# Norms x3 and x4 by halves of the tokens, residual added by matmul, and attention's values and scores in a new order

## The reference

```python
def second_block(x, ...):
    h = x
    for i in range(2):
        mix = gated_deltanet(h, ...) if i == 0 else moba_attention(h, b_w_qkv, b_w_out)
        h = layer_norm_2(ALPHA * h + mix, ln1_g[i], ln1_b[i])                       # x3, x5
        h = layer_norm_2(ALPHA * h + swiglu(h, f_w13[i], f_w2[i]), ln2_g[i], ln2_b[i])  # x4, output
    return h

def swiglu(x, w13, w2):
    g, u = split(x @ w13, 2)
    return (silu(g) * u) @ w2            # hidden width 2816 = 22 x 128

# attention at 256 tokens: 8 heads of 128; rotary on the first 32 dimensions of q and k;
# s = q k^T / sqrt(128), causal; p = softmax(s); o = p v; out = o @ w_out
```

## Time and profile before

| | |
|---|---|
| runs | 1166.37, 1163.05, 1165.20 us; median 1165.2 |
| profiled execution, on the device | 1170.1 us |
| its span, from first to last instruction | 1168.3 us |
| busy PE / PEld / DVE / ACT | 1115.2 / 1066.6 / 802.1 / 614.5 us |
| matmul records | 8328 |
| mean granted TensorE clock | 0.971 of full speed |
| read from memory | 192.9 MB, 166 GB/s over the span |

### The profile page before, as it was taken

How to read it: one execution, slowest core, us unless ns; L and a number is a source line. 1 busy time by engine, 2 the same in 40 slices (tenths; PEclk the granted TensorE clock), 3 DMA queues, 4 the chain that set the end, 5 groups by cost and what they waited for, 6 DMA issues and landing times.

```text
span 1168.3 us, 20107 instructions
## 1 busy us (share of the span) xinstructions
PE 1115.2 (95%) x8328; PEld 1066.6 (91%) x8328; DVE 802.1 (69%) x1355; ACT 614.5 (53%) x1029; POOL 3.3 (0%) x13
## 2 busy tenths in 40 slices
PE   7998989999999998879989999999999999999997
PEld 7998879899999988779989999999999787999996
DVE  7987478878787787486665665555579737555555
ACT  6567435465556547843344454545455546445453
POOL 0000000000000000000000000000000000000000
PEclk8999979999999998889989999999999999999999
DMA  9985246347766623143223265555526424555520
GB/s 374 418 316 166 86 145 252 109 157 244 246 209 203 205 72 127 26 130 134 73 91 100 67 218 194 186 194 188 191 76 201 158 101 157 200 192 181 196 75 37
DMA packets 58554, 195.56 MB, mean 167 GB/s; under 512 B 10848, under 2 KB 11232, under 8 KB 58208
## 3 DMA queue, kind: packets, MB, share of 16 engines
q1 hardware_dynamic: 58464, 194.28, 48.8%
HBM read 192.94 MB, written 1.31 MB: 166 GB/s over the span
## 4 chain that ended last, share of the span: by engine, by line
PE 75%; DVE 16%; ACT 6%; issue 2%; DMA 1%; SPq 1%; ACTq 0%; DVEq 0%
PE ps L534 62%; DVE lo L1639 4%; PE ps L809 4%; ACT hi L1106 2%; DVE raw L1626 2%; PE ps L636 2%; PE ps L541 1%; DVE B L1648 1%; DVE ev L1877 1%; PE ps L553 1%; DVE ev L1874 1%; DVE st L1656 1%; PE ps L691 1%; PE ps L815 1%; DVE B L1661 1%
## 5 line engine op out<-in xcount | busy, mean ns | idle before, releaser
L1639 DVE TENSOR_TENSOR lo<-raw,hi 128x1024 fp32r<-128x1024 f32 x311 | 377.8, 1222 | 170.0 <-ACT hi L1106 169.2
L534 PE MATMUL ps<-hh,hi 128*128 128x256 f32 x1664 | 478.2, 287 | 14.2 <-DVE hl L1673 3.2
L534 PE MATMUL ps<-hl,hi 128*128 128x256 f32 x1664 | 471.5, 283 | 0.0
L534 PE MATMUL ps<-hh,lo 128*128 128x256 f32 x1664 | 471.1, 283 | 0.0
L1106 ACT ACTIVATE hi<-raw 128x1024 fp32r<-128x1024 f32 x311 | 324.4, 1052 | 62.9 <-PE ps L534 62.6
L534 PEld LDWEIGHTS ps<-hh,hi 128*128 128x128 f32 x1664 | 320.0, 192 | 18.6 <-issue 8.7
L534 PEld LDWEIGHTS ps<-hl,hi 128*128 128x128 f32 x1664 | 320.0, 192 | 1.0
L534 PEld LDWEIGHTS ps<-hh,lo 128*128 128x128 f32 x1664 | 319.8, 192 | 0.0
L534 PE MATMUL ps<-fh,hi 128*128 128x256 f32 x392 | 111.4, 284 | 3.5 <-ACT B L1210 2.5
L534 PE MATMUL ps<-fl,hi 128*128 128x256 f32 x392 | 110.2, 281 | 0.0
L534 PE MATMUL ps<-fh,lo 128*128 128x256 f32 x392 | 110.1, 281 | 0.0
(11 more groups left out here) (280 smaller groups left out, 1283.1 us busy)
## 6 DMA issues: line engine op xcount, KB each, us to landing
raw<-in_w SPq DMA_DIRECT2D x359, 512.0 KB, 4.1
B<-in_t SPq DMA_DIRECT2D x2, 512.0 KB, 4.4
xa<-in_x SPq DMA_DIRECT2D x1, 1024.0 KB, 11.2
B<-in_r SPq DMA_DIRECT2D x1, 1024.0 KB, 5.5
out<-h SPq DMA_DIRECT2D x4, 256.0 KB, 2.0
cst<-in_c SPq DMA_DIRECT2D x1, 864.0 KB, 9.1
B<-between SPq DMA_DIRECT2D x32, 4.0 KB, 1.6
vec<-in_v SPq DMA_DIRECT2D x1, 328.5 KB, 7.5
```

The costliest lines, as they stand in the source:

```text
L534: m = g.matmul(o, l, r, start=first and n == 0, stop=last and n == 2, skip_group_check=True)
L1639: g.tensor_tensor(lo[:, j % SPLIT, :], raw[:, PLACE[j] % RAW, :], hi[:, j % SPLIT, :].bitcast(F), ALU.subtract).then_inc(*up("lo", j))
```

## The change

- **Norms x3 and x4** are made by `norm_tokens` as x5 is, on all engines; `after`, `residual` and the filler matmuls inside go. The second feed-forward layer becomes `ffn_tokens` with eight new units `w13r0`. `high` and `low` of the third last `w20` unit + AHEAD are added at its end, as units follow it in the plan.
- **gout**: the residual x2 is multiplied into banks 0 to 3 (`residual_in`) after the last `gdn` tile, then the eight units are done by tokens, units 5 to 7 for c = 0 first.
- **Banks**: in the delta rule banks 0 to 3 and 4 to 7 change places.
- **Attention**: after x4, `absorb` with `vt` 0 to 3 only; then tiles 0 to 11, `scores` 0 and 1, tiles 12 and 13, `scores` 2 and 3, tiles 14 and 15, `scores` 4 and 5, `vt` 4 and 5, `scores` 6 and 7, `vt` 6, `turned` 0 and 1, `vt` 7, `turned` 2 and 3, `apply` 0, `turned` 4, `apply` 1, `turned` 5, all of `carry_in`, then `bout`. A table `ATT` fixes the rotation of the four banks. ScalarE loads the Exp table after the copy of tile 11 and does `exps` between the copies. On VectorE the copies of the values stand behind `weights` 6 and 7.

The diff, cut to its core:

```diff
+ATT = ([("tile", n) for n in range(12)] + [("s", 0), ("s", 1), ("tile", 12), ("tile", 13), ("s", 2), ("s", 3)]
+       + [("tile", 14), ("tile", 15)] + [("s", n) for n in (4, 5, 6, 7)] + [("t", n) for n in range(4)]
+       + [("a", 0), ("t", 4), ("a", 1), ("t", 5), ("a", 2), ("t", 6), ("a", 3), ("t", 7)] + [("a", n) for n in (4, 5, 6, 7)])
+ATT_BANK = {what: 4 + i % 4 for i, what in enumerate(ATT)}
...
+    w += [("vt", k) for k in range(4)] + [("qkv", t) for t in range(16)] + [("vt", k) for k in range(4, 8)]
+    w += [("bout", k) for k in range(8)]
+    w += swiglu(1)
...
-BY_TOKENS = ("x5",)
+BY_TOKENS = ("x3", "x4", "x5")
...
+            def residual_in():
+                for n in (21, 22, 23):
+                    s.wait_ge(*at("conv4", n))
+                s.wait_ge(*at("qss", 2))
+                for k in range(8):
+                    carry_in("x2", k)
+
             def gout(k):
-                rows_in("gout", k, 4, xh[:, k, :], xl[:, k, :], at("gl", k // 2), k == 0, k == 7,
-                        [at("conv4", n) for n in (21, 22, 23)] + [at("qss", 2)] if k == 0 else [])
+                for n, cs in [(k, (0, 1) if k < 5 else (0,))] + ([(5, (1,)), (6, (1,)), (7, (1,))] if k == 7 else []):
+                    rows_out_of("gout", n, (fh if n < 4 else hh)[:, n, :], (fl if n < 4 else hl)[:, n, :], at("gl", n // 2), cs,
+                                n == 7)
...
-            after("x3", lambda k: at("res", ("x3", k - k % 2)))
-            ffn("w130", "w20", "x3", at("hl", ("x3", 0)))
-            after("x4", lambda k: at("res", ("x4", k - k % 2)))
+            ffn_tokens("w130", "w20", "w13r0", "x3", [[at(*core_bank.out[4 + 2 * c + half]) for half in range(2)] for c in range(2)])
+
+            absorb("vt", "x4", [[at("ff_out", ("w130", 2 * FF - 4 + 2 * c + half)) for half in range(2)] for c in range(2)])
...
+            for n in range(12):
+                qk_tile(n)
+            for hd in (0, 2):
+                scores(hd)
+                scores(hd + 1)
+                qk_tile(12 + hd)
+                qk_tile(13 + hd)
+            scores(4)
+            scores(5)
+            vt(4)
+            vt(5)
+            scores(6)
+            scores(7)
+            vt(6)
             turned(0)
             turned(1)
+            vt(7)
+            turned(2)
+            turned(3)
+            apply(0)
+            turned(4)
+            apply(1)
+            turned(5)
+            for k in range(8):
                 carry_in("x4", k)
...
# ScalarE
+                high(UNIT[kdown, FF - 3] + AHEAD)
...
+            for n in range(16):
+                high(UNIT["qkv", n] + AHEAD)
+                s.wait_ge(*at("unit", UNIT["qkv", n]))
+                dst = qq[:, n, :] if n < 8 else kk_[:, n - 8, :]
+                g.activation(dst, bank[ATT_BANK["tile", n]][:, 0:S], ACT.Copy).then_inc(*up("qk_out", n))
+                if n == 11:
+                    table(ACT.Exp)
+                if n in (13, 15):
+                    exps(n - 13)
+                    exps(n - 12)
+            high(UNIT["vt", 4] + AHEAD)
+            high(UNIT["vt", 5] + AHEAD)
+            exps(4)
+            exps(5)
+            high(UNIT["vt", 6] + AHEAD)
+            exps(6)
+            exps(7)
             turned(0)
             turned(1)
+            high(UNIT["vt", 7] + AHEAD)
+            turned(2)
+            turned(3)
...
# VectorE
+            for n in range(16):
+                low(UNIT["qkv", n] + AHEAD)
+                if n in (2, 4, 6, 8):
+                    rope(qq, n - 2)
+                if n in (12, 14):
+                    scores(n - 12)
+                    scores(n - 11)
+                if n in (10, 12, 14):
+                    rope(kk_, n - 10)
+                if n == 14:
+                    weights(0)
+                    weights(1)
+            low(UNIT["vt", 4] + AHEAD)
+            scores(4)
+            scores(5)
+            rope(kk_, 6)
+            weights(2)
+            weights(3)
+            low(UNIT["vt", 5] + AHEAD)
+            low(UNIT["vt", 6] + AHEAD)
+            scores(6)
+            scores(7)
+            weights(4)
+            weights(5)
+            low(UNIT["vt", 7] + AHEAD)
+            weights(6)
+            weights(7)
             s.wait_ge(*at("unit", UNIT["vt", 7]))
             for b in (2, 3):
                 g.tensor_copy(vv[:, 1, (b - 2) * 512:(b - 2) * 512 + 512], bank[b][:, :]).then_inc(*up("v_v", b))
-            weights(6)
-            weights(7)
```

More of the change, by code:

```diff
@@ L741, in absorb @@
                 for k in range(4):
[L742 to L745, removed]
+                    tokens_unit(kind, nid, k, 1)
             def ffn_tokens(kup, kdown, kr, nid, frees):
@@ L1094, in tensor @@
                 bout(k, (1,))
-            ffn_tokens("w131", "w21", "w13r1", "x5", [[at(*a_free[4 + 2 * c + half]) for half in range(2)] for c in range(2)])
+            ffn_tokens("w131", "w21", "w13r1", "x5", [[at("att_lo", 4 + 2 * c + half) for half in range(2)] for c in range(2)])
         def scalar(g, s):
@@ L1524, in gout @@
             def gout(k):
-                high(UNIT["gout", k] + AHEAD)
+                if k < 6:
+                    high(UNIT["gout", k] + AHEAD)
             def nothing(*a):
@@ L1560, in exps @@
                              accum_out=x[:, 3:4]).then_inc(*up("exp", (hd, 1)))
[L1562 to L1576 removed]
             def turned(hd):
[L1579 removed]
+                b = ATT_BANK["t", hd]
                 s.wait_ge(*at("probT_mm", hd))
@@ L2194, in gout @@
             def gout(k):
-                low(UNIT["gout", k] + AHEAD)
+                if k < 6:
+                    low(UNIT["gout", k] + AHEAD)
             def nothing(*a):
@@ L2203, in vector @@
                          "gate": gate, "gturn": gturn, "gout": gout})
-            def after(nid, kind, gain, bias, i, parts=True, b0=0):
-                residual(nid, kind, b0)
-                center(nid, xa, 8, B[0], B[1], 4)
-                root(nid)
-                if parts:
-                    norm_parts(nid, B[1], veccol(gain, i), veccol(bias, i), xa)
-                else:
-                    norm_out(nid, 8, B[1], veccol(gain, i), veccol(bias, i), xa)
-            after("x3", ("gout", 7), "ln1_g_2", "ln1_b_2", 0, b0=4)
-            ffn("w130", "w20", False)
-            after("x4", ("w20", FF - 1), "ln2_g_2", "ln2_b_2", 0)
+            norm_tokens("x3", ("gout", 7), veccol("ln1_g_2", 0), veccol("ln1_b_2", 0), UNIT["w13r0", 2])
+            ffn_tokens("w130", "w20", "w13r0")
+            norm_tokens("x4", ("w20", FF - 1), veccol("ln2_g_2", 0), veccol("ln2_b_2", 0), UNIT["vt", 2])
+            for k in range(4):
+                low(UNIT["vt", k] + AHEAD)
             def rope(dst, n):
```

232 lines of the change are left out of this document (80 added, 152 removed).

## The result

| | before | after |
|---|---|---|
| median of the runs, us | 1164.77 (1161.14 to 1167.33, 6 runs) | 1157.33 (1154.6 to 1161.26, 6 runs) |
| profiled execution, us | 1170.11 | 1159.28 |
| its span, us | 1168.3 | 1157.5 |
| its mean granted clock | 0.971 | 0.979 |

The ratio is 0.9939, with a 95% interval of 0.9912 to 0.9966: faster by 7.4 us. The prediction was 7.3 us, from 1165.2 to 1157.9.

A forecast was written before the change was run, and what follows sets the result against it. TensorE's queue was taken as the bound. Residual +3.5, norm x3 with second layer -5.5, norm x4 -10.8 and attention +5.5 gave -7.3 us, from 1165.2 to 1157.9, with an 8-in-10 range of 1151.5 to 1165.0.

The forecast's parts named there:

- Residual x2: Ahead of `gout`: carrying the residual into the banks is hidden by nothing, +3.5 us, at most 5.2 at partly lower clock.
- lower clock outside attention: Sign of being wrong: the profile after shows TensorE's clock lowered anywhere but in attention; no size given.
- `gout` by halves: Delta rule's output: units 5 to 7 emitted by halves, eight units of 12 matmuls as before, cost nothing.
- Norm x3 and the second layer: Second feed-forward layer and its norm take the last layer's form and time: 197.7 becomes 192.2 us, -5.5.
- norm x4: Norm before attention: 13.88 us becomes 3.1, with values units 0 to 3 covering the second half, -10.8.
- Attention: Same work in a new order, 106.1 us; waits of 7.0 plus slow clock 2.8, less 4.3 before: +5.5 us.
- The waits: TensorE idle before `scores` 2, 4, 6 and `apply` 0 in attention: 1.6, 0.3, 1.6 and 3.6 us, together 7.0.
- The slow clock behind the fourth: Attention, behind the wait before `apply` 0: 2.8 us lost, as after a wait of 3.42 us.
- The table: ScalarE's change to Exp in attention: 1.80 us with the copy before; a drain would make the first wait 1.3 longer.
- B: Rival, chance 0.15: the wait before `apply` 0 is not there, giving 1151.5 us.
- C: Rival: clock falls at unfilled turns x3, x4 and both 1.6 us waits; 1164.9 us (chance 0.17) or 1169.1, slower (0.06).
- D: Rival, chance 0.04: halves do not hide norms x3 and x4, head start of 4.2 us lost twice, +8.4, 1166.3.

The follow-up runs named there:

- experiment 4: Kernel after without the 32 matmul records that carry residual x2 into the banks of `gout`, so the output lacks it: 1153.28 us, ratio 0.9912.
- experiment 11: Kernel after, unchanged, run again: 1155.39 us, ratio 0.9925.
- experiment 5: Kernel after with the last three units of `gout` and `w20` made for both token halves together instead of half 0 first: 1164.23 us, ratio 1.0006.
- experiment 2: Kernel after with all sixteen key and query tiles first, then `vt` 4 to 7 each with two `scores`, and early value copies: 1150.69 us, ratio 0.9893.
- experiment 6: Kernel before without the 14 and 38 idle matmuls in norms x3 and x4: 1169.2 us, ratio 1.005.
- experiment 7: Kernel of experiment 2 with the carry of residual x4 ahead of `apply` 0 instead of behind `turned` 5: 1149.52 us, ratio 0.9883.
- experiment 10: Kernel after with the Exp table loaded behind tile 12 instead of tile 11: 1155.37 us, ratio 0.9929.
- experiment 1: Kernel after with the value copies ahead of `weights` 6 and 7 on VectorE and of `turned` 2 and 3 on ScalarE: 1151.34 us, ratio 0.9899.
- experiment 3: Kernel after with 24 filler matmuls in the wait before `apply` 0: 1155.98 us, ratio 0.9932.
- experiment 8: Kernel of experiment 7 with filler matmuls at four waits of the delta rule, 26 of them before kk(0): 1147.28 us, ratio 0.9862.
- experiment 9: Kernel of experiment 8 without the 26 filler matmuls before kk(0): 1147.95 us, ratio 0.9862.

## Why the prediction was right, step by step

- **Residual x2, +3.5.** Right: 3.7 by experiment 4. In the profile after, the carry itself took 5.20 at a clock of 0.67, the upper bound that was given. It is no further loss: the slow stretch behind the wait had fallen on `gout` 0 in the kernel before. When the clock stayed up (experiment 11), the stretch of `gout` took 32.31. The clock below 1.00 at this place is not the "lower clock outside attention" that the prediction named as a sign of being wrong: it was there before.
- **"`gout` by halves: nothing."** Off by 0.3. A unit of one half gives its follower 1.4 us of cover instead of 2.8, and `gout` 6 waits 0.26 us for its own `hl` part, which VectorE makes just in time.
- **Norm x3 and the second layer, -5.5; norm x4, -10.8.** Right to 0.1: taking the last layer as the measure of the second was sound, since its form and queue order are the same. Experiment 5 shows that 7.2 of it rest on the head start of half 0, and experiment 2 that these two, with the residual, are worth 11.7 (9.0 to 13.6) by the time of the runs too. The other edits in the norms, the tokens' form and the next layer's units for one half at a time, were not tried apart. One reading was loose: of the 13.00 us busy in the norm not most were fillers, but about half (7.00 are left in experiment 6).
- **Attention, +5.5.** 5.2 measured, but the terms were less good than their sum. The waits were 1.51, none, 1.54 and 3.27 us (predicted 1.6, 0.3, 1.6, 3.6): 6.3 instead of 7.0. The slow clock behind the fourth cost 1.7 us (3.35 us at 0.58 and the next 3.7 at 0.92), not 2.8: the term was taken from the stretch behind 3.42 us, which lasted longer. That stretch is a poor measure in any case: behind the same wait the clock stayed at 1.00 in experiments 2, 7, 10 and 11 (last section). Against these 1.8 too much stand 1.5 too little in the work: 104.40 less 6.3 and 1.7 is 96.4 for what was summed up as 94.9 (106.1 less four units). Experiments 1 and 2 say the same, 107.4 and 107.3 for the 106.1. Of it 0.9 can be seen: two units between two pairs of `scores` take 5.98 us (896.58 to 902.56) and not 5.60, three times over, 1.1 in all; the `scores` themselves take 0.58, 0.07 less than counted, 0.6 in all; and the first twelve tiles take 34.0 instead of 33.6. Nearly all of the 0.38 lies at the two changes of kind: from the last start of a tile to the first of `scores` it is 0.31 (902.25 to 902.56), from the first start of a tile behind `scores` to its second 0.30 (896.58 to 896.88), where inside a tile it is 0.12. The two errors had opposite signs, and the total owes its 0.3 to that.
- **The table.** 1.40 us from the load to the next `hi` (887.35 to 888.75), 1.80 from the copy before, as in the earlier trace rows. The figure with a drain that the Trainium skill (ScalarE: Activation LUTs, What ACT_TABLE_LOAD costs) states would have made the first wait an estimated 2.9. It is not borne out: the wait was 1.51.
- **The rivals.** B did not come true (the fourth wait was 3.27). C did not: behind the turns and behind both waits of 1.5 the clock stayed at 1.00. D did not; experiment 5 shows that it was a real danger, of 7.2 us. C had its ground all the same: in another place the clock fell behind waits as short as 1.14 us (below). So that it stayed up behind the waits of 1.5 is what the runs show, and not something that the prediction could derive; it had rows on both sides and took "nothing" as an assumption.

What was not argued and could have been: the scores between the keys are a loss, 1.8 us in W to B once the copies are early. They put VectorE's `rope` on TensorE's path, where the values could have covered it (experiment 2).

## What to carry to other kernels

The end of a norm, or of any other statistics between two matmul stages, is hidden by making the last units of the stage half by half, so that one half's statistics run beside the other half's matmuls; count the head start in microseconds (4.2 left 0.83 us idle here, 1.4 left 2.7 and a slow clock behind it, 7.2 us for two norms). Interleaving an operation early is only a gain if what it needs from the slower engines is ready: lay the queues side by side, and put the work that needs nobody (values, residual) in front of the work that does. A stage that exists in the same form elsewhere in the trace is the best price list for one that is to be rewritten; it was right to 0.1 us twice here.

## What the runs showed of the hardware

- In attention the granted clock didn't fall behind waits of 1.4 to 1.65 us, nor behind the idle 0.83 us of the turns, in any profile of these kernels. Behind the 2.27 us of the kernel before it fell (0.66 over the next 5 us). Behind the wait of 3.24 to 3.28 us before `apply` 0 it fell in all five that have it (after, 4, 5, 10, 11), and not where 3.1 us of fillers left 0.40 (3).
- The length of a wait doesn't settle it. Behind the wait of 3.42 to 3.46 us before kk(0) in the delta rule the clock fell in before, after, 1, 3, 4, 5, 6, 8 and 9, and stayed at 1.00 in 2, 7, 10 and 11. After and 11 are the same kernel; here they are, the wait and the 6.80 us from its end:

```profile
478.76 2.93 PE L816 MATMUL ps<-B 128*128 128x128 f32 x16 [3.44 <-ACT B L1457]
478.76:485.56 6.80, 6.80 (x33) 6.03 (x34) 5.01 (x11) 6.04 (x11) 0.00 (x0) 0.75 0.00 0
...
475.89 2.05 PE L816 MATMUL ps<-B 128*128 128x128 f32 x16 [3.45 <-ACT B L1457]
475.89:482.69 6.80, 5.74 (x37) 4.92 (x37) 5.01 (x11) 6.77 (x13) 0.00 (x0) 1.00 0.00 0
```

- Ahead of the residual x2 too it was both: the 32 matmuls took 3.81 us behind waits of 0.94, 1.02, 1.03 and 1.05 us, and 5.44 behind 1.14, 1.14, 1.26 and 1.31; but behind 1.61 us they took 3.81 in experiment 8 and 5.27 in experiment 9, and in the kernel before the clock fell behind 1.03. What decides it, no run here tells.
- A slow stretch costs what it loses only where TensorE sets the pace: behind norm x3, 2.4 lost on TensorE were 1.7 of time (experiment 6); inside the delta rule 2.4 were 0.4 (7 against 8); and behind kk(0) they were nothing: from its start to the end of the next wait of both (L542, released by ScalarE's activation at L1377) are 23.00 us in after, with the clock at 0.75 over the first 6.8, and 23.01 in 11, with 1.00 (478.76 to 501.76, 475.89 to 498.90).
- Between executions of one kernel the time goes with the mean granted clock: the kernel before took 7 to 8 us less at 0.987 than at 0.974. That is as much as this whole change, so a single pair of executions can't tell it.
